# Squares and norms of the projection straight from PSUM, head gains folded into the rotary tables

## What is computed

```python
u = _rmsnorm(h, g_attn[l])
proj = u @ w_in[l]
qa, ka, va, qd, kd, vd = [proj[..., offs[i]:offs[i + 1]] for i in range(6)]
qa = _rope(_rmsnorm(qa.reshape(B, L, SWA_HQ, SWA_DH), g_q_swa[l]), pos)
ka = _rope(_rmsnorm(ka.reshape(B, L, SWA_HKV, SWA_DH), g_k_swa[l]), pos)
# the same for the halves of qd and kd with g_q_diff, g_k_diff and heads of 32

def _rope(x, pos):
    ...
    x1, x2 = xf[..., : d // 2], xf[..., d // 2:]
    out = jnp.concatenate([x1 * cos - x2 * sin, x2 * cos + x1 * sin], axis=-1)
```

## Time and profile before

| | |
|---|---|
| median of 3 runs | 2652.1 us (2647.63 to 2661.2) |
| profiled execution | 2657.38 us, its span 2655.7 us |
| mean granted clock of PE | 0.946 |
| PE, DVE, ACT, POOL busy | 90%, 68%, 54%, 18% of the span |
| `project` | from 0 to about 282 us; its first product with heads starts at 83.8 |

### The profile page before, as it was taken

How to read it: one execution, slowest core, us unless ns; L and a number is a source line. 1 busy time by engine, 2 the same in 40 slices (tenths; PEclk the granted TensorE clock), 3 DMA queues, 4 the chain that set the end, 5 groups by cost and what they waited for, 6 DMA issues and landing times. The chain is left out here.

```text
span 2655.7 us, 34895 instructions
## 1 busy us (share of the span) xinstructions
PE 2384.2 (90%) x10781; PEld 1757.1 (66%) x10782; DVE 1808.3 (68%) x2225; ACT 1446.8 (54%) x1687; POOL 490.4 (18%) x578
## 2 busy tenths in 40 slices
PE   6999698999989479999999899999999999999970
PEld 5768565555445257777778677777777777777750
DVE  4698456999745367676865576666766668687756
ACT  4222355888711166565754575655665557577550
POOL 0466100111102302121211121111111111122120
PEclk9999798999999689999999999999999999999985
DMA  4233802233015288686965686766776669599769
GB/s 152 64 102 102 173 13 88 55 64 65 1 69 95 81 311 309 238 317 225 350 227 203 214 312 248 272 232 224 274 279 223 230 223 350 212 338 336 272 225 379
DMA packets 254996, 540.87 MB, mean 204 GB/s; under 512 B 28528, under 2 KB 60528, under 8 KB 253952
## 3 DMA queue, kind: packets, MB, share of 16 engines
q1 hardware_dynamic: 232736, 501.10, 56.1%
q0 software_dynamic: 20880, 34.49, 3.5%
q10 hardware_dynamic: 1296, 4.19, 0.4%
HBM read 513.63 MB, written 60.15 MB: 216 GB/s over the span
## 5 line engine op out<-in xcount | busy, mean ns | idle before, releaser
L1712 DVE TENSOR_TENSOR wlo<-raw,whi 128x2048 fp32r<-128x2048 f32 x387 | 881.6, 2292 | 355.8 <-ACT whi L1597 354.8
L1597 ACT CAST whi<-raw 128x2048 fp32r<-128x2048 f32 x387 | 736.9, 1913 | 269.0 <-PE gl_ps L1867 149.3
L1869 PE MATMUL gl_ps<-whi,xt_hi 128*128 128x512 f32 x1056 | 429.4, 407 | 56.4 <-ACTq L1660 36.4
L1870 PE MATMUL gl_ps<-wlo,xt_hi 128*128 128x512 f32 x1056 | 421.9, 400 | 0.0
L1871 PE MATMUL gl_ps<-whi,xt_lo 128*128 128x512 f32 x1056 | 421.0, 399 | 0.0
L1869 PEld LDWEIGHTS gl_ps<-whi,xt_hi 128*128 128x128 f32 x1056 | 204.8, 194 | 108.9 <-issue 60.7
L1871 PEld LDWEIGHTS gl_ps<-whi,xt_lo 128*128 128x128 f32 x1056 | 204.4, 194 | 44.5
L1533 POOL CAST sel<-onehot 128x128 fp32r (+1 forms) x66 | 47.7, 724 | 1005.0 <-PE gl_ps L1875 759.7
L1870 PEld LDWEIGHTS gl_ps<-wlo,xt_hi 128*128 128x128 f32 x1056 | 205.2, 194 | 41.8
L1869 PE MATMUL y_ps<-whi,ht_hi 128*128 128x512 f32 x512 | 208.8, 408 | 0.0
L1870 PE MATMUL y_ps<-wlo,ht_hi 128*128 128x512 f32 x512 | 202.6, 396 | 0.0
(11 more groups left out here) (260 smaller groups left out, 3784.2 us busy)
## 6 DMA issues: line engine op xcount, KB each, us to landing
raw<-in_w_mlp SPq DMA_DIRECT2D x390, 1024.0 KB, 5.1
yk<-y_dram SPq DMA_DIRECT2D x7, 2048.0 KB, 26.6
k_st<-qk_dram SPq DMA_DIRECT2D x32, 260.0 KB, 7.4
xs<-in_x SPq DMA_DIRECT2D x16, 512.0 KB, 4.6
w_in_raw<-in_w_in SPq DMA_DIRECT2D x32, 256.0 KB, 3.0
q_st<-qk_dram SPq DMA_DIRECT2D x32, 256.0 KB, 6.8
qk_dram<-qk_hi SPq DMA_DIRECT2D x24, 256.0 KB, 2.5
qk_dram<-qk_lo SPq DMA_DIRECT2D x24, 256.0 KB, 3.1
```

The source lines that it names most:

```text
L1597: act.copy(whi[:, k % SPL, :], raw[:, k % RAW, :]).then_inc(hi_done, 1)
L1712: dve.tensor_tensor(wlo[:, k % SPL, :], raw[:, k % RAW, :], whi[:, k % SPL, :].bitcast(F32), ALU.subtract).then_inc(lo_done, 1)
L1869: pe.matmul(bank, xh[:, half, kc, :], hi, start=start, stop=False, skip_group_check=True)
L1870: pe.matmul(bank, xh[:, half, kc, :], lo, start=False, stop=False, skip_group_check=True)
```

## The change

ACT squares straight from `pp` to `sq`; the copy `pr` and POOL's square are gone. DVE multiplies `pp` with the reciprocals. A table `rope_gain` holds cosine times gain and sine times gain for all blocks, built by POOL once per group (two slots). With it DVE's cosine and POOL's sine are one product of the full width each, and `t2` holds sine times its own half, so difference and sum take the other half. `rotate` moves from the end of DVE's iteration m to its start (item m - 2 still), POOL has only sines and tables. `high_qk`, `low_qk` and the stores run for item m - 3, the transposes for m - 2, and the loops end one iteration earlier. The weight ring has 13 slots instead of 14, so `LATE` is 3. PE waits for the norm (`qn_done`) before it uses a bank again. The 16-row block of the rotary table is cleared first, and SP's load of it waits for that.

```diff
-        RAW, RING, GW = 4, 14, 512
+        RAW, RING, GW = 4, 13, 512
...
-        pr = sb("pr", [P, 2, GW])
+        table = sb("rope_gain", [P, 2, 2, T * DH])
...
+        def rope_gain(i, part):
+
+            r, w, d = heads(i)[0:3]
+            g, t = items[i]
+            return table[0:r, g % 2, part, t * d:(t + 1) * d].unsqueeze(1).broadcast_to((r, w // d, d))
...
+            sp.wait_ge(rope_set, 1)
...
-                    h = i - FH
-                    if h >= 2:
-                        act.wait_ge(qn_done, h - 1)
-                        act.wait_ge(sq_done, h - 1)
-                    act.copy(pr[0:r, h % 2, 0:w], pp[0:r, i % 4, 0:w]).then_inc(proj_out, 1)
+                    h, w = i - FH, heads(i)[1]
+                    if h >= 1:
+                        act.wait_ge(hs_done, h)
+                    act.activation(sq[0:r, 0:w], pp[0:r, i % 4, 0:w], ACT.Square).then_inc(sq_done, 1)
+                    if g == NG - 1:
+                        act.copy(v_all[0:r, t, 0:128], pp[0:r, i % 4, 128:256]).then_inc(proj_out, 1)
...
-                if FH <= m - 4 < NI:
-                    high_qk(m - 4)
+                if FH <= m - 3 < NI:
+                    high_qk(m - 3)
...
-                    dve.wait_ge(t2_done, 2 * (h - 1))
-                dve.tensor_tensor(split_heads(qn[0:r, h % 2, 0:w], d), split_heads(pr[0:r, h % 2, 0:w], d),
+                    dve.wait_ge(t2_done, h - 1)
+                    dve.wait_ge(t1_done, h - 1)
+                dve.tensor_tensor(split_heads(qn[0:r, h % 2, 0:w], d), split_heads(pp[0:r, i % 4, 0:w], d),
...
-                r, w, d, _, c = heads(i)
-                h, nh, t = i - FH, w // d, items[i][1]
-                dve.wait_ge(gain_done, h + 1)
+                r, w, d = heads(i)[0:3]
+                h = i - FH
+                dve.wait_ge(qn_done, h + 1)
+                dve.wait_ge(table_done, 4 * items[i][0])
                 if h >= 1:
                     dve.wait_ge(ro_done, 2 * h)
-                q, x, y, o = (split_halves(b, d) for b in (qn[0:r, h % 2, 0:w], t1[0:r, 0:w], t2[0:r, 0:w], ro[0:r, h % 2, 0:w]))
-                cos = rope[0:r, t, c:c + d // 2].unsqueeze(1).broadcast_to((r, nh, d // 2))
-                for s in range(2):
-                    ins = dve.tensor_tensor(x[:, :, s, :], q[:, :, s, :], cos, ALU.mult)
-                ins.then_inc(t1_done, 1)
+                dve.tensor_tensor(split_heads(t1[0:r, 0:w], d), split_heads(qn[0:r, h % 2, 0:w], d), rope_gain(i, 0), ALU.mult
+                                  ).then_inc(t1_done, 1)
+                x, y, o = (split_halves(b, d) for b in (t1[0:r, 0:w], t2[0:r, 0:w], ro[0:r, h % 2, 0:w]))
                 dve.wait_ge(t1_done, h + 1)
-                dve.wait_ge(t2_done, 2 * (h + 1))
+                dve.wait_ge(t2_done, h + 1)
                 if h >= 2:
                     dve.wait_ge(qk_ps, h - 1)
-                dve.tensor_tensor(o[:, :, 0, :], x[:, :, 0, :], y[:, :, 0, :], ALU.subtract).then_inc(ro_done, 1)
-                dve.tensor_tensor(o[:, :, 1, :], x[:, :, 1, :], y[:, :, 1, :], ALU.add).then_inc(ro_done, 1)
+                dve.tensor_tensor(o[:, :, 0, :], x[:, :, 0, :], y[:, :, 1, :], ALU.subtract).then_inc(ro_done, 1)
+                dve.tensor_tensor(o[:, :, 1, :], x[:, :, 1, :], y[:, :, 0, :], ALU.add).then_inc(ro_done, 1)
...
-                if FH <= m - 4 < NI:
-                    low_qk(m - 4)
+                if FH <= m - 2 < NI:
+                    rotate(m - 2)
+                if FH <= m - 3 < NI:
+                    low_qk(m - 3)
...
-                if FH <= m - 2 < NI:
-                    rotate(m - 2)
...
-            def squares(i):
-                r, w = heads(i)[0:2]
-                h = i - FH
-                pool.wait_ge(proj_out, i + 1)
-                if h >= 1:
-                    pool.wait_ge(hs_done, h)
-                if items[i][0] == NG - 1:
-                    pool.tensor_copy(v_all[0:r, items[i][1], 0:128], pr[0:r, h % 2, 128:256])
-                pool.tensor_tensor(sq[0:r, 0:w], pr[0:r, h % 2, 0:w], pr[0:r, h % 2, 0:w], ALU.mult).then_inc(sq_done, 1)
-            def gain_and_sine(i):
-                r, w, d, gain, c = heads(i)
-                h, nh, t = i - FH, w // d, items[i][1]
+            pool.wait_ge(rope_set, 1)
+            def make_table(g):
+                d, gain = groups[g][3:5]
+                c, n = (0 if d == DH else 2 * 32), d // 2
+                gains_of = (gains if d == DH else gaind)[:, gain, :]
+                for part in range(2):
+                    out = table[:, g % 2, part, 0:T * d].rearrange("p (t s n) -> p t s n", t=T, s=2)
+                    for s in range(2):
+                        half = gains_of[:, s * n:(s + 1) * n].unsqueeze(1).broadcast_to((P, T, n))
+                        pool.tensor_tensor(out[:, :, s, :], rope[:, :, c + part * n:c + (part + 1) * n], half, ALU.mult
+                                           ).then_inc(table_done, 1)
+            def sine(i):
+                r, w, d = heads(i)[0:3]
+                h, g = i - FH, items[i][0]
                 pool.wait_ge(qn_done, h + 1)
-                v = split_heads(qn[0:r, h % 2, 0:w], d)
-                table = gains if d == DH else gaind
-                pool.tensor_tensor(v, v, table[0:r, gain, :].unsqueeze(1).broadcast_to((r, nh, d)), ALU.mult).then_inc(gain_done, 1)
-                pool.wait_ge(gain_done, h + 1)
+                pool.wait_ge(table_done, 4 * g)
                 if h >= 1:
                     pool.wait_ge(ro_done, 2 * h)
-                q, y = split_halves(qn[0:r, h % 2, 0:w], d), split_halves(t2[0:r, 0:w], d)
-                sin = rope[0:r, t, c + d // 2:c + d].unsqueeze(1).broadcast_to((r, nh, d // 2))
-                for s in range(2):
-                    pool.tensor_tensor(y[:, :, s, :], q[:, :, 1 - s, :], sin, ALU.mult).then_inc(t2_done, 1)
-            for m in range(FH + 1, NI + 5):
-                if FH <= m - 1 < NI:
-                    squares(m - 1)
-                if FH <= m - 2 < NI:
-                    gain_and_sine(m - 2)
+                pool.tensor_tensor(split_heads(t2[0:r, 0:w], d), split_heads(qn[0:r, h % 2, 0:w], d), rope_gain(i, 1), ALU.mult
+                                   ).then_inc(t2_done, 1)
+                if i == first_of[g] and 2 <= g < NG - 1:
+                    make_table(g + 1)
+            make_table(1)
+            make_table(2)
+            for i in range(FH, NI):
+                sine(i)
...
-                        pe.wait_ge(proj_out, m - 3)
+                        h = m - 4 - FH
+                        if h < 0:
+                            pe.wait_ge(proj_out, m - 3)
+                        else:
+                            pe.wait_ge(qn_done, h + 1)
+                            if items[m - 4][0] == NG - 1:
+                                pe.wait_ge(proj_out, FH + m - 3 - first_of[NG - 1])
...
-                if FH <= m - 3 < NI:
-                    transpose_qk(m - 3)
+                if FH <= m - 2 < NI:
+                    transpose_qk(m - 2)
```

More of the change, by code:

```diff
@@ L138, in project @@
         sq_done, hs_done, hstd_done = sem("head_squares"), sem("head_sums"), sem("head_std")
-        qn_done, gain_done, t1_done, t2_done, ro_done = (sem("qn_done"), sem("gain_done"), sem("t1_done"),
-                                                        sem("t2_done"), sem("rotated"))
+        qn_done, table_done, t1_done, t2_done, ro_done = (sem("qn_done"), sem("table_done"), sem("t1_done"),
+                                                         sem("t2_done"), sem("rotated"))
         qk_ps, hi_done, lo_done = sem("qk_transposed"), sem("hi_done"), sem("lo_done")
+        rope_set = sem("rope_set")
         qk_stored = [sem(f"qk_stored{i}") for i in range(2)]
@@ L216, in _ @@
                 load_w(p)
-            for m in range(NI + 5):
+            for m in range(NI + 4):
                 if m + 3 < T:
@@ L222, in _ @@
                         load_w(p + RAW)
-                if FH <= m - 4 < NI:
-                    store(m - 4)
+                if FH <= m - 3 < NI:
+                    store(m - 3)
             for i in range(2):
@@ L311, in _ @@
             step = chained(dve, dve_chain)
+            dve.memset(rope[:, NT, :], 0.0).then_inc(rope_set, 1)
             dve.memset(eps[:, :], EPS).then_inc(consts_set, 1)
@@ L483, in _ @@
             transpose_u(0)
-            for m in range(NI + 3):
+            for m in range(NI + 2):
                 if m < NI:
```

## The result

| | before | changed |
|---|---|---|
| median of 20 runs each, us | 2660.64 (2647.63 to 2663.67) | 2641.43 (2634.11 to 2658.98) |
| profiled execution, its span, us | 2657.38, 2655.7 | 2640.58, 2638.9 |
| mean granted clock | 0.946 | 0.948 |
| first to last product with heads | 83.81 to 273.32 = 189.51 | 83.31 to 260.79 = 177.48 |
| last product to last store issued | 6.62 | 4.87 |

The ratio is 0.9936 with a 95% interval of 0.9923 to 0.995: 17.0 us faster, between 13.3 and 20.5, or 0.64% (the two medians lie 19.2 apart).

The account below looks back on a forecast made before the run. PE's stops, every one ended by a late DVE, and the tail were taken as the bound. Gains 3.97 + 1.55 + 4.92 + 1.4 + 1.9 = 13.7, less 0.7, gave 13.0: 2652.1 - 13.0 = 2639.1 us, range 2633 to 2653.

Parts of the forecast that it names:

- PE's losses: Projection: time PE loses against its beat of 6.01 us an item, at three borders and inside group 2; sum 13.6 us.
- the 3.97, 1.55 and 4.92: PE's losses in us at the border to group 2, inside group 2 and at the border to group 3, all counted as gain.
- group 4: Border to group 4 and the iterations behind it: 3.2 us lost before, 1.2 to 1.8 after, gain 1.4.
- Square on ACT, no copy: Projection: one ACT instruction replaces another of the same width, the hand-over to POOL goes, nothing is late.
- turn 2.0 instead of 2.74: DVE's rotation, from cosine to `ro`: 2.0 us, bounds 1.4 and 2.2, replacing the cosine pair's 2.74.
- DVE's item: DVE's time per item in the projection: 5.2 us, with a weight chunk 5.84, both under PE's 6.01.
- Norm from PSUM: DVE's norm product reading PSUM instead of SBUF: 0 us more, bounds 0 and 0.1.
- Tables: POOL's table products of 288, some 0.8 us each, at the first item of groups 2 and 3; DVE delayed 2 us a table.
- the 0.7 I took off: Deduction from the summed gain for DVE's lag at the borders left by table building: 0.7 us, bounds 0 to 3.
- Ring: 13 slots instead of 14: borders to groups 2 and 3 cost nothing while DVE's lag is under 1.3 us.
- Tail: From the last product to the last store issued, 6.6 us before: gain 1.9, bounds 1.2 and 2.5.
- C: Rival: Square and Sqrt need different ACT tables, two loads of 1.28 us an item, some 18 us slower, 2670; chance 0.04.

Follow-up runs that it names:

- e11: Changed kernel with the rotation back at the end of DVE's iteration, transposes and later steps one iteration later, ring of 14: first to last product 176.17 us, ratio to before 0.9928.
- e2: Kernel before with only ACT's square from PSUM and the norm from PSUM: first to last product 177.07 us, ratio 0.9924.
- e9: Changed kernel, but ACT copies first and squares the copy, and DVE norms from the copy: first to last product 178.28 us.
- e1: Changed kernel with ACT's copy, POOL's square and the norm from the copy back; tables, order and ring kept: first to last product 193.46 us, ratio to before 1.0009.
- e7: Changed kernel with a weight ring of 12 slots, four late chunks: first to last product 178.41 us.
- e8: Changed kernel profiled once more, unaltered: first to last product 177.62 us, next stage's first load at 268.85.
- e6: Changed kernel with the weight ring of 14 slots back, normed heads kept in another buffer: first to last product 177.13 us.
- e10: Changed kernel with an unused 512-wide square on POOL behind each sine: first to last product 190.08 us.

## Why the prediction came out as it did

**The time.** 2639.1 was predicted, 2641.43 measured, inside the range; 2644.4 against 2640.58 for the profiled execution. That the median is so near is luck in part: the predicted gain was 13.0, the measured one 17.0 (19.2 between the medians), and the kernel before has 2660.64 over 20 runs, not the 2652.1 of three. Two errors nearly cancelled, a start 8.5 too low and a gain 6.2 too small by the medians (4.0 by the ratio). My chances had "within 0.5%" as the likeliest with 0.50 and "faster" at 0.41; the interval begins at 13.3, just at that bound, and its middle lies beyond.

**PE's losses: right.** That only PE's stops and the tail are worth anything held in every kernel. With PE 6.01 apart over both borders, the 3.97, 1.55 and 4.92 are gone in full. In group 4 the iterations are 3.56, 4.11 and 3.33 long now, against 3.3 in e11 where nothing stops them: 1.1 lost, just under the 1.2 to 1.8; by the same beat about 2.8 were lost before instead of 3.2. Gain 1.6 for 1.4. Sum 12.04, measured body 12.03.

**The step that failed: the square.** "Square on ACT, no copy ... so nothing is late" priced the copy's replacement and left POOL's side at nothing. I read the 2.74 of the cosine pair as a quarrel with the gain product alone, although the square's row, ending as the gain's begins, was on the same stretch. By e2 and e9 moving the square is the whole 12 us; by e1 the folding of the scales without it lengthens the body by 4 us in the one profile, and leaves the total where it was (1.0009). The size of the step "turn 2.0 instead of 2.74" came out right (1.94), since the changed kernel has neither the square nor the halves, but the reason given for it would have sent a reader to the wrong half of the change. What the tables give DVE is the shorter chunk (0.60; predicted 0.62, in e2 still 0.83) and 1.3 of tail.

**DVE's item** 5.2 and 5.84 predicted, 5.27 and 5.87 measured. **Norm from PSUM** at nothing: 691 ns in the mean over 24 norms, against 692 from SBUF in e9. The Trainium skill ("VectorE: DVE Perf Modes", section on the TRN2 errata) would have a PSUM source cost more; these two figures don't bear that out for this operation, which has one input in PSUM and one in SBUF.

**Tables.** Each product of 288 took 0.97 in the mean of eight, not 0.8, but the cost to DVE was less: the two `ro` take 144.25 to 146.09 = 1.84 instead of 0.68, so 1.2 instead of 2. The lag it leaves was gone before the next border, and the 0.7 I took off for it had nothing behind it. Without it the sum would have been 13.7 and past the 13.3.

**Ring:** the cover at the borders to groups 2 and 3 held, and with more room than said, since with 12 slots PE still didn't stand there for `w_in_lo` (e7); only the border to group 4 is crossed. **Tail:** 1.9 predicted, 1.75 measured, 0.41 of it from the squares (e2), the rest from tables and order. **Table loads of ACT** (C): none.

**What stays open.** 14.3 of the 17.0 us lie in `project`. In the two profiles the rest, 2.5, lies in later stages whose code is the same: the three from window attention to the routing together 2.8 longer, the experts 5.8 shorter (1675.1 and 1669.3 from their first weight load to the first instruction of the stage behind them), the last one 0.4 longer. e8 repeats the shorter time of the changed kernel (1670.0), but over the kernels above, whose experts are identical, that stretch takes from 1663.5 (e6) to 1680.7 (e7), so a few profiles can't say whether the 2.7 are a consequence or scatter, and the interval holds 14.3 as well.

## What to carry to other kernels

To price an operation that is moved off an engine, look not at that engine's share of the span but at whose instructions start late or run long beside it: POOL was busy 18% of the span, yet 37.01 of the 53.2 us of this stretch, and its square of some 1.05 us held DVE up by 0.78 an item, and that was 12 us. What a stage costs is then read from the slowest engine's item against the bound's beat, with signs: 5.27 against 6.01 absorbs chunks, the two borders and tables, 6.05 against 6.01 absorbs nothing. Where a change has two halves, price each half without the other before adding them up; a sum can be right while its parts are credited to the wrong edit.

## What the runs showed of the hardware that I had not expected

- DVE's and POOL's elementwise operations with two SBUF inputs exclude each other for most or all of an instruction in these rows, and the one that starts first has it. The `ro` difference took 0.42 alone and 1.19 with POOL's square started 0.13 before it (e10); POOL's sine took 1.28 alone (e11) and 1.80 when DVE's `t` had started 0.05 before it, while that `t` took 0.69. In e1 and e10 DVE, which waits for the sine's signal, lost in nearly every full-width item to the square that stood next in POOL's own queue. The Trainium skill ("SBUF — State Buffer", section "SBUF: two separate sides") describes the pair of ports behind this as an exclusive lock, taken by a DVE operation with two SBUF inputs against a GpSimd operation that reads SBUF, for the whole instruction; e10's rows agree to within 0.14: `ro` ends 0.28 after the square.
- A lag may keep itself; this is argued from rows, no run isolates it. In the changed kernel an item's last product is over when the transposes start (130.05), and `ro` of the item before starts at 129.96, so a square waiting for ACT's copy would come behind `ro` and miss it. In e1 DVE is late, the copy lies ready, the square meets `ro`, and 6.05 an item keeps DVE late.
- A stop of PE costs more than its length where the clock falls behind it, but it did not fall behind each one. In e10 the four us from 134 around a stop of 0.88 show 1.00, and those from 194 around one of 3.11 show 0.71: first row. In e1 those behind one of 3.10 (198.15) show 1.00, second row, and those around one of 4.38 (251.41) 0.62. With transposes 6.01 apart as the measure, the stop of 3.11 cost 5.1 us and that of 3.10 cost 3.5. What tells the two apart these rows don't say.

```profile
194.00:198.00 4.00, 3.08 (x9) 2.42 (x10) 3.59 (x8) 0.31 (x1) 0.00 (x0) 0.71 0.39 111
198.00:202.00 4.00, 3.85 (x19) 3.18 (x20) 3.56 (x8) 1.66 (x4) 0.37 (x1) 1.00 0.62 166
```
